# Four stages of a two-block network changed, and attention's outputs scaled in place of its probabilities

## The chip, the cores and the metric

One core of one Trainium2 chip. The time is the device time of one execution in microseconds.

## The reference

A sequence of 512 tokens of width 1024 goes through two blocks of two layers each. Both layers of the first block project the normed input, mix it in three ways side by side, and end with a feed-forward part:

```python
y_a, v_first = rwkv7_mixer(p_a, ...)      # state per head: S*w + sa (kk*a) + v k;  y = S r
# y is centred and scaled per head: (y - mean) * rsqrt(var + eps) * gn_w + gn_b
y_b = retention_mixer(p_b, positions)
y_c = mla_mixer(p_c, ...)                 # 8 heads: softmax(q k) @ v, causal
h = h + mix @ w_out[l]
h = h + (silu(gate) * up) @ w_down[l]
```

The second block has an even layer (rg_lru with gates sigmoid(u @ gate_w + b), 2 x 2 matrices of 128x128 for each of 8 heads, and a short convolution) and an odd layer (gated linear attention; its input gives q and k of 512 columns each). All is float32.

## The kernel before

Activations stand transposed: 128 features by 512 tokens in a tile of the arena, A(n); R(n) is the same memory as fp32r. A large product is made from two parts of each operand, high (ScalarE's rounded copy) and low (VectorE's difference): `product` issues three fp32r matmuls (L705 to L707). `gemm` (L731) is a plain fp32 product, which the trace shows as two records. Weights come in slabs of up to 128x2048 through two ring places; `prepare` splits a slab on ScalarE (L1555) and VectorE (L2142), and a slab may take a ring place of parts when the products of the slab two before it are done (slab_group). Each engine runs an order written out by hand; PSUM banks rotate, and `group` waits until the bank's last reader has released it.

What the change touches, in order of time:

- Start: TensorE's first product waits for the first half slab's parts (L2254).
- Attention, `mla(l)`: 32 units (8 heads, 4 blocks of queries). TensorE computes unit u's scores, VectorE their maximum in place (L2400, the custom operation), ScalarE the exponential with the row sums (L1699). VectorE then takes the sum's reciprocal (L2411) and scales the unit (L2413); three units later TensorE transposes it (L867), waiting for rows_scaled; ScalarE or VectorE (T_OWNER) copies it out, and `attended` (L845) multiplies with the values per pair of heads. VectorE's scans for rwkv stand after units 8 and 16, and a subtraction after unit 24. Behind the loop come kks (the sums behind L1683's squares), retention's scores with VectorE's masks (L2463), and `removal_key` between the two halves of these masks.
- rwkv: `token_tiles` turns the values (L1001); at the end ymean, a subtraction (L2588), squares (L1785), yvar. `beside(n)` places n products of the output projection.
- Even layer, `rg_gates(m)`, m = 0 to 7: four fp32 products.
- Between the layers: the last even_out tile and the odd layer's input are done in two token halves (`last_output`, `half_root`, `odd_input`). Products with odd_qk0's columns stand beside the parts of each k, those with odd_qk1's behind them; odd_qk1 is split in the ring amid odd_input.

## Time and profile before

| | us |
| --- | --- |
| median of 3 runs | 1994.52 (1991.6 to 1994.92) |
| the profiled execution | 1991.63, its span 1989.8 |
| TensorE busy (matmuls) | 1934.5, 97% of the span, 12070 instructions |
| VectorE busy | 1100.2, 55% |
| ScalarE busy | 832.7, 42% |
| HBM | 82 GB/s over the span |

Times in the rows are us from the span's start. PE is TensorE, DVE VectorE, ACT ScalarE, POOL GpSimd, SP the DMA queue's engine. Matmul records overlap: their ends are modelled, and the distance from start to start tells the rate.

### The profile page before, as it was taken

The page shows a single profiled execution, that of the slowest core. Times are in us where ns is not written, and L with a number is a line of the kernel's source. Part 1 is how long each engine was busy: PE and PEld are TensorE (multiplying, and loading weights), DVE is VectorE, ACT ScalarE, POOL GpSimd, SP SyncE. Part 2 cuts the span into 40 slices and gives each one's busy share as a digit, 9 for nine tenths or more (in the row PEclk, how much of TensorE's full clock was granted, in tenths as well). Part 3 has the DMA queues.
Part 4 walks back from the last instruction along what each step waited for, and adds up shares of the span by engine and source line. Part 5 has one row for each costly group of instructions (what it writes and reads, how often), then busy time and mean ns, then how long its engine had stood idle before and what let it go on. Part 6 is the DMA issues. An engine that isn't in the chain of part 4 may idle for free.

```text
span 1989.8 us, 28365 instructions
## 1 busy us (share of the span) xinstructions
PE 1934.5 (97%) x12070; PEld 1562.4 (79%) x12070; DVE 1100.2 (55%) x1585; ACT 832.7 (42%) x1206; POOL 41.7 (2%) x34
## 2 busy tenths in 40 slices
PE   7999899999999999998999999999999999999998
PEld 6875678888888888657788888887787777799887
DVE  6567846543444544876644334457676674443474
ACT  5257534322223313773432222245554653335273
POOL 0100000000000000000000000000000000020000
PEclk9999999999999999999999999999999999999999
DMA  6240003322322323201132233233212222212102
GB/s 236 94 125 1 24 24 106 106 80 101 106 99 73 114 88 111 63 1 46 64 106 93 84 109 106 73 108 127 101 69 106 85 74 96 100 63 95 64 16 81
DMA packets 28268, 170.01 MB, mean 85 GB/s; under 512 B 3632, under 2 KB 3888, under 8 KB 12912
## 3 DMA queue, kind: packets, MB, share of 16 engines
q1 hardware_dynamic: 28144, 168.21, 24.4%
q8 instruction: 96, 1.57, 0.3%
q14 instruction: 28, 0.23, 0.0%
HBM read 161.77 MB, written 2.10 MB: 82 GB/s over the span
## 4 chain that ended last, share of the span: by engine, by line
PE 88%; DVE 7%; ACT 3%; issue 1%; DMA 0%; SPq 0%; DVEq 0%; ACTq 0%
PE accumulators L705 26%; PE accumulators L707 25%; PE accumulators L706 25%; PE accumulators L731 4%; DVE ring_low L2142 1%; ACT arena L1652 1%; PE accumulators L845 1%; DVE accumulators L2400 1%; ACT ring_high L1555 1%; DVE arena L2413 1%; DVE arena L2463 1%; PE accumulators L1420 1%; PE accumulators L1439 1%; PE accumulators L953 1%; PE accumulators L987 1%
## 5 line engine op out<-in xcount | busy, mean ns | idle before, releaser
L705 PE MATMUL accumulators<-arena_split,ring_high 128*128 128x512 f32 (+1 forms) x2212 | 864.4, 391 | 18.2 <-DVE ring_low L2254 10.4
L706 PE MATMUL accumulators<-arena_split,ring_high 128*128 128x512 f32 (+1 forms) x2212 | 852.4, 385 | 0.0
L707 PE MATMUL accumulators<-arena_split,ring_low 128*128 128x512 f32 (+1 forms) x2212 | 852.4, 385 | 0.0
L705 PEld LDWEIGHTS accumulators<-arena_split,ring_high 128*128 128x128 f32 x2212 | 416.7, 188 | 110.6 <-DVE ring_low L2254 10.4
L706 PEld LDWEIGHTS accumulators<-arena_split,ring_high 128*128 128x128 f32 x2212 | 416.8, 188 | 86.0 <-issue 4.8
L707 PEld LDWEIGHTS accumulators<-arena_split,ring_low 128*128 128x128 f32 x2212 | 416.7, 188 | 83.5
L1555 ACT ACTIVATE ring_high<-ring 128x2048 fp32r<-128x2048 f32 (+3 forms) x161 | 281.5, 1749 | 405.5 <-PE accumulators L707 403.6
L2142 DVE TENSOR_TENSOR ring_low<-ring,ring_high 128x2048 fp32r<-128x2048 f32 (+3 forms) x161 | 336.9, 2093 | 185.5 <-ACT ring_high L1555 184.8
L1573 ACT ACTIVATE arena<-accumulators 128x512 f32<-128x512 f32 x72 | 43.1, 598 | 277.2 <-DVE accumulators L2123 277.1
L2123 DVE TENSOR_TENSOR accumulators<-accumulators,rstd 128x512 f32<-128x512 f32 x72 | 50.3, 699 | 118.8 <-PE accumulators L707 118.8
L2622 DVE TENSOR_TENSOR arena<-arena,accumulators 128x512 f32<-128x512 f32 x44 | 30.3, 688 | 119.6 <-PE accumulators L707 118.1
L2149 DVE TENSOR_TENSOR arena_split<-arena,arena_split 128x512 fp32r<-128x512 f32 x94 | 62.1, 690 | 53.8 <-ACT arena_split L1561 53.6
L731 PE MATMUL accumulators<-arena 128*128 128x512 f32 (+8 forms) x256 | 85.3, 482 | 2.5 <-DVE arena L2463 2.5
L1523 ACT ACTIVATE arena<-accumulators 128x512 f32<-128x512 f32 (+1 forms) x76 | 43.3, 596 | 93.5 <-PE accumulators L707 50.3
L705 PE MATMUL accumulators<-ring_high,arena_split 128*128 128x352 f32 (+2 forms) x240 | 82.1, 342 | 0.0
L707 PE MATMUL accumulators<-ring_high,arena_split 128*128 128x352 f32 (+2 forms) x240 | 80.9, 337 | 0.0
L706 PE MATMUL accumulators<-ring_low,arena_split 128*128 128x352 f32 (+2 forms) x240 | 80.8, 337 | 0.0
L731 PEld LDWEIGHTS accumulators<-arena 96*128 96x128 f32 (+2 forms) x256 | 38.3, 189 | 30.9 <-issue 16.5
L1561 ACT ACTIVATE arena_split<-arena 128x512 fp32r<-128x512 f32 x94 | 55.4, 622 | 17.0 <-DVE arena L2596 6.5
L2117 DVE TENSOR_TENSOR arena<-accumulators,rstd 128x512 f32<-128x512 f32 x40 | 27.6, 689 | 46.6 <-PE accumulators L707 46.5
L1567 ACT ACTIVATE arena<-h 128x512 f32<-128x512 f32 x32 | 20.1, 629 | 66.5 <-DVE h L2193 66.5
L705 PEld LDWEIGHTS accumulators<-ring_high,arena_split 128*128 128x128 f32 x240 | 45.0, 188 | 3.6 <-issue 0.2
(362 smaller groups left out, 1722.0 us busy)
## 6 DMA issues: line engine op xcount, KB each, us to landing
ring<-slabs_in SPq DMA_DIRECT2D x115, 1024.0 KB, 4.8
ring<-slabs_in SPq DMA_DIRECT2D x38, 704.0 KB, 4.0
ring<-slabs_in SPq DMA_DIRECT2D x4, 576.0 KB, 3.5
h<-x_in SPq DMA_DIRECT2D x4, 512.0 KB, 7.6
con<-con_in SPq DMA_DIRECT2D x1, 2048.0 KB, 9.3
arena<-arena SPq DMA_DIRECT2D x8, 256.0 KB, 4.1
arena<-arena SPq DMA_DIRECT2D x32, 64.0 KB, 2.5
out<-arena SPq DMA_DIRECT2D x8, 256.0 KB, 2.0
```

Of the source, the lines that this page charges most:

```text
L705: pe.matmul(out, weight[0], right[0], start=start, stop=False)
L706: pe.matmul(out, weight[0], right[1], start=False, stop=False)
L707: return pe.matmul(out, weight[1], right[0], start=False, stop=stop)
L731: mm = pe.matmul(b[out_rows, 0:N], w, r, start=(k == 0), stop=(k == len(weights) - 1))
L1523: f(dst, b[rows, 0:n], func, scale=scale).then_inc(cnt.up(act_released), 1)
L1555: f(ring_high[:, n % SLOTS, 0:cols], ring[:, at % SLOTS, 0:cols], ACT.Copy).then_inc(cnt.up(slab_high_ready), 1)
L1561: f(R(dst), src, ACT.Copy).then_inc(cnt.up(high_ready), 1)
L1573: f(dst, bank(key)[:, :], ACT.Silu).then_inc(cnt.up(act_released), 1)
L2123: tt(b[:, :], b[:, :], rstd[:, :], MUL).then_inc(cnt.up(scaled_ready), 1)
L2142: tt(ring_low[:, n % SLOTS, 0:cols], ring[:, at, 0:cols], ring_high[:, n % SLOTS, 0:cols].bitcast(F32), SUB).then_inc(cnt.up(slab_split), 1)
L2149: tt(R(dst), src, R(high).bitcast(F32), SUB).then_inc(cnt.up(parts_ready), 1)
L2622: tt(a, A(j % 2)[:, 0, :], b[:, :], MUL).then_inc(cnt.up(dve_released), 1)
```

## The change

Five edits. (1) VectorE writes a tile of zeros first, and TensorE multiplies it with itself seven times (ZERO_PRODUCTS = 7) into the last bank, before its first product. (2) The gates' weights and inputs are split into high and low parts, held in three tiles over the decay constants, and `rg_gates` uses `split_gemm`. (3) rwkv's values are turned by a product with a centring matrix (identity minus the mean over 64) in place of a transpose; the mean's sums and subtraction go, and squares are taken from PSUM. (4) odd_qk1 is split early, into half tiles of the arena in place of the ring (`early_high`, `early_low`), and all four banks are filled k by k. (5) The probabilities aren't scaled. For each pair of heads VectorE writes 512 reciprocals of the sums (4 blocks x 2 heads x 64 equal columns), TensorE transposes them (`spread_factors`), ScalarE copies them out, and VectorE multiplies the pair's output with them as it leaves PSUM (`scaled_values`). VectorE now also copies the transposed third block.

The diff, cut to its core (plain lines of context and new semaphores are left out):

```diff
@@ -128,6 +128,7 @@
     put("ones64", same)
+    put("centre64", np.eye(P) - same / RW_HD)
...
@@ -366,7 +367,9 @@
         arena_split = nc.alloc_sbuf_tensor_at("arena_split", [P, 53, T], F32R, offset=arena_at)
+        con_at = nc.sbuf_base
         con = sb("con", [P, NCON])
+        gate_parts = nc.alloc_sbuf_tensor_at("gate_parts", [P, 3, T], F32R, offset=-(-(con_at + 4 * CON["decay"][0]) // 32) * 32)
...
@@ -612,7 +628,12 @@
         TOKENS = (slice(0, T // 2), slice(T // 2, T))
-        T_OWNER = ("dve", "act", "act", "act")
+        def half_weights(places, k):
+            tile, at = places[k // 2]
+            return R(tile)[:, at + k % 2 * P:at + k % 2 * P + P]
+        T_OWNER = ("dve", "act", "dve", "act")
...
@@ -845,8 +866,17 @@
                     if blocks[-1] == NT - 1:
-                        enter(key, "act")
+                        enter(key, "dve")
                         mm.then_inc(psum_ready, 1)
+                def spread_factors(pair_of):
+                    pe.wait_ge(sums_inverted, cnt.next(sums_inverted))
+                    b = group(("factor", l, pair_of), "act")
+                    for j in range(NT):
+                        js = slice(j * P, (j + 1) * P)
+                        mm = pe.transpose(b[:, js], A(4 + pair_of)[:, 0, js], cst("ident"))
+                    mm.then_inc(psum_ready, 1)
...
@@ -860,7 +890,7 @@
                         w = u - 3
-                        pe.wait_ge(rows_scaled, cnt.next(rows_scaled))
+                        pe.wait_ge(*taken(("s", l, w)))
...
@@ -868,6 +898,9 @@
                         attended((u - 13) // 8, VALUE_UNITS[(u - 13) % 8])
+                    if u >= 12 and u % 8 == 4 and u < len(units):
+                        spread_factors((u - 12) // 8)
+                spread_factors(MLA_H // 2 - 1)
...
@@ -1003,7 +1036,12 @@
                 pe.wait_ge(values_ready, cnt.next(values_ready))
-                token_tiles(0, 14)
+                for hp in range(2):
+                    b = group(("tok", l, 0, hp), "act")
+                    for j in range(NT):
+                        js = slice(j * P, (j + 1) * P)
+                        mm = pe.matmul(b[:, js], A(14 + hp)[:, 0, js], cst("centre64"), start=(j == 0), stop=(j == NT - 1))
+                    mm.then_inc(psum_ready, 1)
...
@@ -1124,16 +1162,16 @@
                 mm.then_inc(outputs_ready, 2)
-                beside(2)
+                beside(3)
+                pe.wait_ge(y_squares_ready, cnt.next(y_squares_ready, 2))
                 for hp in range(2):
-                    for s in range(2):
-                        pe.wait_ge(*taken(("y", l, s)))
-                    gemm(("ymean", l, hp), "dve", rows, [cst("ones64")], [A(49 + hp)[:, 0, :]])
-                beside(1)
-                for hp in range(2):
-                    pe.wait_ge(y_squares_ready, cnt.next(y_squares_ready))
+            pe.wait_ge(zeros_ready, 1)
+            zeros = A(50)[:, 0, :]
+            for n in range(ZERO_PRODUCTS):
+                pe.matmul(banks[BANKS - 1][:, :], zeros[:, 0:P], zeros, start=True, stop=True)
...
@@ -1232,14 +1270,10 @@
             def rg_gates(m):
-                if m < 2:
-                    pe.wait_ge(first_gates_loaded, 16)
-                else:
-                    pe.wait_ge(gates_loaded, 16)
-                pe.wait_ge(conv_ready, cnt.next(conv_ready))
+                pe.wait_ge(gate_parts_ready, cnt.next(gate_parts_ready, 2))
                 for n in range(4):
-                    w = A(m)[:, 0, n * P:(n + 1) * P]
-                    gemm(("gate_ri", m, n // 2, n % 2), "act", rows, [w], [A(19 + m % 2)[:, 0, :]])
+                    w = gate_part(GATE_HIGH)[:, n * P:(n + 1) * P], R(m)[:, n * P:(n + 1) * P]
+                    split_gemm(("gate_ri", m, n // 2, n % 2), "act", [w], [(gate_part(INPUT_HIGH), gate_part(INPUT_LOW))])
...
@@ -1280,15 +1314,16 @@
             for n in range(4):
-                w = split_tiles(split_slab("odd_qk0"), n % 2 * DT * P, DT) if n < 2 else None
+                if n < 2:
+                    w = split_tiles(split_slab("odd_qk0"), n % 2 * DT * P, DT)
+                else:
+                    pe.wait_ge(slab_split, split_index["odd_qk1"] + 1)
+                    w = [(half_weights(QK1_HIGH, n % 2 * DT + k), half_weights(QK1_LOW, n % 2 * DT + k)) for k in range(DT)]
                 bk, w = held[n]
-                if w is None:
-                    w = split_tiles(split_slab("odd_qk1"), n % 2 * DT * P, DT)
-                    held[n] = bk, w
...
@@ -1296,24 +1331,13 @@
-            for k in range(DT):
-                parts_step(k)
-                for n in range(2):
-                    odd_product(n, 0, k)
-                if k == 2:
-                    half_norm_sum(1)
-            later = [(n, half, k) for half in range(2) for k in range(DT) for n in (2, 3)]
-            for n, half, k in later[:2 * DT]:
-                odd_product(n, half, k)
-            del later[:2 * DT]
-            for k in range(DT):
-                parts_step(k)
-                for n in range(2):
-                    odd_product(n, 1, k)
-                if k < 4:
-                    odd_product(*later.pop(0))
-            for n, half, k in later:
-                odd_product(n, half, k)
+            for half in range(2):
+                for k in range(DT):
+                    parts_step(k)
+                    for n in range(4):
+                        odd_product(n, half, k)
+                    if half == 0 and k == 2:
+                        half_norm_sum(1)
...
@@ -1688,9 +1712,8 @@
                           ACT.Copy).then_inc(cnt.up(act_released), 1)
-                    last = 14 + max(VALUE_UNITS)
-                    if u >= last and (u - last) % 8 == 0 and (u - last) // 8 < MLA_H // 2 - 1:
-                        copy_out(("pv", l, (u - last) // 8), A(4 + (u - last) // 8)[:, 0, :])
+                    if u >= 13 and u % 8 == 5 and u < MLA_H * NT:
+                        copy_out(("factor", l, (u - 13) // 8), A(4 + (u - 13) // 8)[:, 0, :])
...
@@ -1699,6 +1722,7 @@
+                copy_out(("factor", l, MLA_H // 2 - 1), A(3 + MLA_H // 2)[:, 0, :])
...
@@ -1716,8 +1740,6 @@
                     act.preload_act_table_set(ROOTS)
-                copy_out(("pv", l, MLA_H // 2 - 1), A(3 + MLA_H // 2)[:, 0, :])
...
@@ -1754,6 +1776,7 @@
                     if n == 3:
+                        act.wait_ge(*taken(("pv", l, MLA_H // 2 - 1)))
...
@@ -1778,11 +1801,13 @@
                     b = bank(("y", l, s))
+                    squares = A(51, 2).rearrange("p h (j s t) -> p (h j) s t", s=2, t=RW_CHUNK)
+                    f(squares[:, :, s, :], b[:, :].rearrange("p (j t) -> p j t", t=RW_CHUNK), ACT.Square).then_inc(
+                        cnt.up(y_squares_ready), 1)
+                for s in range(2):
+                    b = bank(("y", l, s))
                     f(dst[:, :, s, :], b[:, :].rearrange("p (j t) -> p j t", t=RW_CHUNK), ACT.Copy).then_inc(cnt.up(act_released), 1)
-                for hp in range(2):
-                    act.wait_ge(*taken(("ymean", l, hp)))
-                    f(A(51 + hp)[:, 0, :], A(49 + hp)[:, 0, :], ACT.Square).then_inc(cnt.up(y_squares_ready), 1)
...
@@ -1873,14 +1898,27 @@
+            def gate_highs(m):
+                if m < 2:
+                    act.wait_ge(first_gates_loaded, 16)
+                else:
+                    act.wait_ge(gates_loaded, 16)
+                f(gate_part(GATE_HIGH), A(m)[:, 0, :], ACT.Copy).then_inc(cnt.up(gate_high_ready), 1)
+                act.wait_ge(conv_ready, cnt.next(conv_ready))
+                f(gate_part(INPUT_HIGH), A(19 + m % 2)[:, 0, :], ACT.Copy).then_inc(cnt.up(gate_high_ready), 1)
                 prepare(f"even_xb_gc{m}")
+                if m == 0:
+                    gate_highs(0)
                     gate_silu(m + 1)
+                    gate_highs(m + 1)
...
@@ -1911,6 +1949,16 @@
+            def early_high(first, last):
+                at = slab_index["odd_qk1"]
+                act.wait_ge(slab_loaded[at % SLOTS], 16 * (at // SLOTS + 1))
+                src = ring[:, at % SLOTS, :].rearrange("p (a t) -> p a t", t=T // 2)[:, first:last]
+                (tile, start), count = QK1_HIGH[first], last - first
+                f(arena_split[:, tile:tile + count, start:start + T // 2] if tile > 25 else
+                  R(tile)[:, start:start + count * T // 2].rearrange("p (a t) -> p a t", t=T // 2), src, ACT.Copy).then_inc(
+                    cnt.up(early_high_ready), 1)
...
@@ -1936,14 +1984,16 @@
+            early_high(5, 7)
+            early_high(7, 8)
             last_output(0)
+            early_high(0, 5)
+            splits.append("odd_qk1")
                     last_output(1)
-                if m == 2:
-                    prepare("odd_qk0")
...
@@ -2154,6 +2204,7 @@
+            dve.memset(A(50)[:, 0, :], 0.0).then_inc(zeros_ready, 1)
...
@@ -2391,6 +2442,13 @@
+                def scaled_values(pair_of):
+                    dve.wait_ge(psum_ready, finished(("pv", l, pair_of)))
+                    dve.wait_ge(*taken(("factor", l, pair_of)))
+                    y = A(4 + pair_of)[:, 0, :]
+                    tt(y, bank(("pv", l, pair_of))[:, :], y, MUL).then_inc(cnt.up(dve_released), 1)
...
@@ -2405,12 +2463,13 @@
                            bank(("t", l, w))[:, 0:(i + 1) * P].rearrange("p (j t) -> p j t", t=P)).then_inc(cnt.up(dve_released), 1)
-                    w = u - 1
-                    if 0 <= w < MLA_H * NT:
-                        dve.wait_ge(*taken(("s", l, w)))
-                        dve.reciprocal(stat[:, 3, w:w + 1], stat[:, 2, w:w + 1]).then_inc(cnt.up(dve_done), 1)
-                        dve.wait_ge(cnt.sem, cnt.value)
-                        ts(probabilities(w), probabilities(w), stat[:, 3, w:w + 1], None, MUL).then_inc(cnt.up(rows_scaled), 1)
+                    if u >= 18 and u % 8 == 2 and (u - 18) // 8 < MLA_H // 2 - 1:
+                        scaled_values((u - 18) // 8)
+                    if u >= 9 and u % 8 == 1:
+                        dve.wait_ge(*taken(("s", l, u - 2)))
+                        factors = A(4 + (u - 9) // 8)[:, 0, :].rearrange("p (j e c) -> p e j c", j=NT, e=2)
+                        sums = stat[:, 2, u - 9:u - 1].rearrange("p (e j) -> p e j", j=NT)[:, :, :, None]
+                        dve.reciprocal(factors, sums.broadcast_to((P, 2, NT, 64))).then_inc(cnt.up(sums_inverted), 1)
...
@@ -2463,6 +2522,7 @@
                     if hp == 0:
+                        scaled_values(MLA_H // 2 - 1)
...
@@ -2582,11 +2642,6 @@
                 for hp in range(2):
-                    dve.wait_ge(psum_ready, finished(("ymean", l, hp)))
-                    b = bank(("ymean", l, hp))
-                    y = A(49 + hp)[:, 0, :]
-                    stt(y, b[:, :], -1.0 / RW_HD, y, MUL, ADD).then_inc(cnt.up(dve_released), 1)
-                for hp in range(2):
...
@@ -2717,10 +2772,20 @@
+            def gate_lows(m):
+                dve.wait_ge(gate_high_ready, cnt.next(gate_high_ready))
+                tt(R(m), A(m)[:, 0, :], gate_part(GATE_HIGH).bitcast(F32), SUB).then_inc(cnt.up(gate_parts_ready), 1)
+                dve.wait_ge(gate_high_ready, cnt.next(gate_high_ready))
+                tt(gate_part(INPUT_LOW), A(19 + m % 2)[:, 0, :], gate_part(INPUT_HIGH).bitcast(F32), SUB).then_inc(
+                    cnt.up(gate_parts_ready), 1)
                 prepare(f"even_xb_gc{m}")
+                if m == 0:
+                    gate_lows(0)
...
@@ -2737,6 +2802,8 @@
                 tt(yb, b[:, :], c, MUL).then_inc(cnt.up(dve_released), 1)
+                if m < DT - 1:
+                    gate_lows(m + 1)
...
@@ -2798,8 +2865,20 @@
+            def early_low(dst, first, last, high):
+                src = ring[:, slab_index["odd_qk1"] % SLOTS, :].rearrange("p (a t) -> p a t", t=T // 2)[:, first:last]
+                dve.wait_ge(early_high_ready, cnt.next(early_high_ready))
+                return tt(dst, src, high.bitcast(F32), SUB)
             last_square(0)
-            odd_input(0, {3: lambda: last_square(1), 4: lambda: prepare("odd_qk0")})
+            as_halves = lambda view: view.rearrange("p (a t) -> p a t", t=T // 2)
+            dve.wait_ge(psum_ready, finished(("eo", DT - 1, 0)))
+            early_low(arena_split[:, 14:16, TOKENS[0]], 5, 7, as_halves(R(24))).then_inc(cnt.up(dve_done), 1)
+            early_low(as_halves(R(25)[:, TOKENS[0]]), 7, 8, as_halves(R(25)[:, TOKENS[1]])).then_inc(cnt.up(dve_done), 1)
+            early_low(arena_split[:, 9:14, TOKENS[0]], 0, 5, arena_split[:, 26:31, TOKENS[0]]).then_inc(cnt.up(slab_split), 1)
+            splits.append("odd_qk1")
+            odd_input(0, {3: lambda: last_square(1)})
```

## Rows read from the trace of the kernel before

**Rows 1.** The page, part 4: shares of the chain that ended last, by engine.

```profile
PE 88%; DVE 7%; ACT 3%; issue 1%; DMA 0%; SPq 0%; DVEq 0%; ACTq 0%
```

**Rows 2.** Waits of TensorE: waiter, awaited: us in all, times, longest.

```profile
PE accumulators L867 <- DVE arena L2413: 6.3, 16, 0.6
```

**Rows 3.** First 17 us, timeline: start, us, engine line operation [idle before, awaited].

```profile
0.81 0.17 DVE L2158 MEMSET epsilon<- 128x1 f32 x5 [0.81 <-PEq L3097]
...
10.39 0.79 PE L705 MATMUL accumulators<-arena_split,ring_high 128*128 128x512 f32 x1 [10.39 <-DVE ring_low L2254]
...
15.64 0.39 PE L705 MATMUL accumulators<-arena_split,ring_high 128*128 128x512 f32 x1
```

**Rows 4.** Chain in time (start, us, what), and VectorE's timeline: one gate stage.

```profile
1469.70 3.43 PE accumulators L731 x8
...
1505.79 3.43 PE accumulators L731 x8
...
1500.57 0.69 DVE L2739 TENSOR_TENSOR arena<-accumulators,arena 128x512 f32<-128x512 f32 x1
```

**Rows 5.** Timeline of TensorE where the odd layer's q and k are projected.

```profile
1732.02 0.35 PE L705 MATMUL accumulators<-arena_split,ring_high 128*128 128x256 f32 x1 [0.63 <-DVE arena_split L2796]
...
1738.88 0.39 PE L705 MATMUL accumulators<-arena_split,ring_high 128*128 128x256 f32 x1 [2.94 <-DVE arena_split L2796]
...
1757.01 0.29 PE L707 MATMUL accumulators<-arena_split,ring_low 128*128 128x256 f32 x1
1757.13 0.28 PE L705 MATMUL accumulators<-arena_split,ring_high 128*128 128x256 f32 x1
...
1761.81 0.50 PE L705 MATMUL accumulators<-arena_split,ring_high 128*128 128x512 f32 x1 [0.20 <-DVE ring_low L2142]
```

**Rows 6.** There: busy times, granted clock (0.50), DMA share, GB/s; then ScalarE, VectorE.

```profile
1740.00:1742.00 2.00, 2.00 (x10) 1.99 (x10) 1.82 (x6) 2.00 (x7) 0.00 (x0) 0.50 0.92 389
...
1757.39 1.92 ACT L1555 ACTIVATE ring_high<-ring 128x2048 fp32r<-128x2048 f32 x1 [5.82 <-PE accumulators L707]
...
1759.35 2.41 DVE L2142 TENSOR_TENSOR ring_low<-ring,ring_high 128x2048 fp32r<-128x2048 f32 x1 [7.57 <-ACT ring_high L1555]
...
1729.53 0.88 DVE L2788 SCALAR_TENSOR_TENSOR arena<-arena,par 128x256 f32<-128x256 f32 x2 [3.38 <-ACT arena L1930]
```

**Rows 7.** Timeline of TensorE in layer 0's rwkv: the means, and the token tiles.

```profile
279.01 1.88 PE L731 MATMUL accumulators<-arena,con 128*128 128x512 f32 x4
...
218.28 1.97 PE L1001 MATMUL accumulators<-con,arena 128*128 128x128 f32 x16
```

**Rows 8.** Two lines' instructions, the reciprocals: count: ns min/median/max, first and last start.

```profile
L2411 DVE RECIPROCAL stat<-stat x64: 152/159/165, 153.4 to 859.4; 128x1 f32<-128x1 f32 x64
...
L2225 DVE RECIPROCAL splus<-splus x1: 253/253/253, 348.1 to 348.1; 128x16 f32<-128x16 f32 x1
```

**Rows 9.** Timelines inside layer 0's attention loop: VectorE, TensorE, VectorE, ScalarE.

```profile
171.89 1.22 DVE L2387 TENSOR_TENSOR_SCAN arena<-con,arena 128x512 f32<-128x512 f32 x1
...
176.28 0.55 PE L867 MATMUL accumulators<-con,arena 128*128 128x128 f32 x3 [0.52 <-DVE arena L2413]
...
178.71 0.57 DVE L2400 CUSTOM_DVE_ANT_0 accumulators<-accumulators,con 128x384 f32<-128x384 f32 x1 [0.52 <-PE accumulators L731]
...
179.90 0.19 ACT L1699 ACTIVATION_READ_ACCUMULATOR arena<-accumulators,stat 128x1 f32 x1
```

**Rows 10.** Timelines behind the attention loops of layers 0 and 1 (from 859).

```profile
192.05 0.19 ACT L1699 ACTIVATION_READ_ACCUMULATOR arena<-accumulators,stat 128x1 f32 x1
...
195.18 1.12 PE L731 MATMUL accumulators<-arena,con 128*128 128x512 f32 x2 [1.33 <-ACT arena L1683]
...
204.38 1.29 DVE L2463 TENSOR_TENSOR arena<-accumulators,con 128x512 f32<-128x512 f32 x2 [1.53 <-PE accumulators L731]
...
859.16 0.19 ACT L1699 ACTIVATION_READ_ACCUMULATOR arena<-accumulators,stat 128x1 f32 x1
...
862.72 0.70 PE L731 MATMUL accumulators<-arena,con 128*128 128x512 f32 x1
```

14 lines of the change are left out of this document (12 added, 2 removed).

## The prediction

> **What bounds the kernel now.** I read four views in this order. The chain of work that ended last says who holds the end: TensorE does, for 88% of the span [rows 1]. So an edit that takes TensorE work away shortens the run by that work, unless a wait takes its place, and the waits of TensorE come next. They are short and few; the group that this change is after is the transposes of attention (L867), which wait 16 times for VectorE's scaling of the probabilities, 6.3 us in all [rows 2]. A record is longer than the slot its matmul takes: 256 columns show 0.28 us at 0.12 us apart [rows 5]. A wait is therefore some 0.16 us longer than its record says, and those 16 waits are worth 6.3 + 16 x 0.16 = 8.9 us. Third, the timeline at the places that the diff touches. Last, the granted clock of the one stretch in which the spacing of equal matmuls doubles.
>
> **Zero products at the start.** TensorE first works at 10.39, when the first half slab is split; twelve matmuls of 512 columns pass before 15.64, from where they stand closer [rows 3]. In the stage of the gates 144 such matmuls take 36.09 - 3.43 = 32.66 us, 0.227 each [rows 4]. The twelve took 5.25 us and would take 2.72 at that rate: **-2.5 us** if the array is awake by then. VectorE writes the zeros ahead of its memset at 0.81 [rows 3], so TensorE starts about 1.2. A plain fp32 product of 512 columns costs 2 x 0.429 = 0.86 us at the full rate (eight records in 3.43 [rows 4]) and twice that at half. Three at 1.71 and four at 0.86 end near 9.8, ahead of 10.39. If the clock never rose they would end at 13.2, and this would be +2.8 instead. What is late next is the next slab, whose transfer and parts have a few us of room; I take the full 2.5. The Trainium skill ("TensorE: Matmul & The Clock Gate", The HAM clock gate) states that the throttled state is the default and activity releases it, which would give the same sum.
>
> **Gates in parts.** For each of eight m, four fp32 products (eight records, 3.43 us) become twelve fp32r ones, 12 x 0.227 = 2.72: -0.71 each, **-5.7 us** in all. It costs two copies on ScalarE and two subtractions on VectorE for each m (0.5 to 0.7 us each). They are in time: VectorE ends its product with gb at 1501.2, the two subtractions would end at 1502.5, and TensorE wants them at 1505.79 [rows 4]. TensorE sets the pace of this stage with no wait at all, so nothing is behind them; without this cover it would be 1.3 us for each m.
>
> **Centred values.** The two sums for the mean of y go, with the VectorE and ScalarE steps that hung on them: 4 records of 0.43, 1.71 us, and some 0.14 of switching [rows 7]. The squares are ready before the three products that now stand beside them are done. In turn, eight of the sixteen transposes at 218.28 become fp32 products of two records each, 8 x 0.11 = 0.87 us, and TensorE goes on to the next step without a wait, so this is on the path. Net -1.0 for each layer, **-2.0 us**. The bounds are -1.85 x 2 (the 0.87 hidden) and 0.
>
> **The qk slab in half tiles.** Before, 64 half products were cut by the split of odd_qk1, which stands in the middle of the parts. TensorE stood 2.94 us before 1738.88 [rows 5], and then ran at a clock of 0.50 of full, the 1.2 GHz level, for some 3.4 us [rows 6]. After, all 192 matmuls run from 1732.02 in one stream: 192 x 0.12 = 23.0, and 0.4 for the norm sum. VectorE's part of a k comes every 1.13 us (0.44 + 0.34 + 0.35), TensorE's takes 1.44, so no wait is left inside. The early split costs VectorE 2.35 us (2.41 us for 2048 columns), which fit into its 3.38 us of idle before 1729.53 [rows 6]. But the new order ends all four banks together. The split of odd_qk2 needs the ring place of odd_qk0, free only when bank qk1 is done, now the last k. From the last matmul of qk1 at 1757.01 it takes 4.80 us until the next pair starts at 1761.81: ScalarE's copy from 1757.39, VectorE's subtraction from 1759.35 [rows 5, 6]. Before, qk2 and qk3 covered that for all but 0.36; now seven matmuls do, 0.84 us. The next pair starts at 1732.02 + 23.4 + 4.80 - 0.84 = 1759.4, so -2.4. An idle time of 3.9 us is longer than the one that ended at 1738.88, and I expect the clock to fall again, half of 3.4 us: +1.7. **-0.7 us**; bounds -2.4 and 0.
>
> **Attention: outputs scaled in place of probabilities.** Per layer, 32 small reciprocals and 32 scalings leave VectorE, and TensorE's transposes wait for the exponential alone: the waits go, -8.9 / 2 = -4.5. Four groups of four transposes come (spread_factors), 0.11 each and 0.1 of switching: three in the loop, +1.5. VectorE gets one reciprocal of 512 elements for each pair of heads. Its price is not in the trace, its slope is: 128x1 takes 159 ns, 128x16 takes 253 [rows 8], (253 - 159) / 15 = 6.3 ns an element, so 159 + 511 x 6.3 = **3.35 us**. The bounds are 0.69 (a product of 512 elements [rows 4]) and 253 / 16 x 512 = 8.1; I take the slope, since both rows are of this operation and share a fixed cost. This is what the change turns on. The scores' maximum of the next unit is queued behind this reciprocal, and TensorE waits for it twice: at the factors' transposes and at the next unit's.
> Unit 17 [rows 9]: VectorE's scan would start 0.6 earlier than 171.89, since the scaling ahead of it is gone. The scan holds the engine 1.1 us, the maximum of unit 17 some 0.35 (256 columns, against 0.57 for the 384 of 178.71), so the reciprocal runs from 172.75 to 176.1. TensorE reaches the factors at 176.28 - 0.68 - 0.43 = 175.2 and stands 1.0. Factors and score end at 177.05. Unit 18's maximum starts at 176.1; from its start to its exponential's end is 1.4 (178.71 to 180.09), so the transposes start near 177.6 and not 176.28: 0.5 more. Pair 2 is like it. For unit 9 fewer products lie between and it stands 2.1 + 0.45. Together 5.5 a layer. The loop: -4.5 + 1.5 + 5.5 = +2.5, +5.0 for two layers.
> Behind the loop: the last reciprocal starts when unit 31's exponential ends (192.24) and ends at 195.6; the factors take until 196.15, and the sums that started at 195.18 come after them, +1.0 [rows 10]. In layer 1 nothing was waited for here, so there is no room to hide in: the exponential ends at 859.35, the reciprocal would end at 862.7, the factors at 863.2, vlow takes 1.83, and the sums that started at 862.72 start at 865.0, +2.3. Then scaled_values of the last pair stands ahead of removal_key on VectorE and waits for pv; VectorE was idle 1.53 us before 204.38, where the next masks start [rows 10]. TensorE ends pv right before the products of those masks, about 1.1 us ahead of 204.38; 203.3 + 0.6 (scaled_values) + 1.35 (removal_key) = 205.25, +0.9 in each layer, and from there VectorE holds the path. Behind the loop +5.1. Attention: **+10.1 us**.
>
> **Sum.** -2.5 - 5.7 - 2.0 - 0.7 + 10.1 = -0.8 us. The profiled execution took 1991.63 us, its span 1989.8, with 1.8 around it; the median of the three shown is 1994.52, and the changes of a span carry over. Profiled 1990.8; against the median **1993.7 us**.
>
> **Rivals.** *The reciprocal is cheap* (a 512-element pass like any other, 0.69): no stall is left in the loop, -6.0 for two layers; behind it -1.0 (the squares come earlier), +0.5 and 2 x 0.9, +1.3. Attention -4.7, the sum -15.6, 1978.9 us. Against it stands the slope of 6.3 ns, where a product of 512 elements takes 1.3 an element. *The stalls cost the clock, slower*: TensorE stands 2.1 us at unit 9 and 2 us before the last factors, in each layer, where now it stands 0.5 at most and 1.5. If half the rate follows each of the four, as after 1738.88, that is 4 x 1.7 = +6.8: 2000.5 us. It decides from the point at which 2 us of standing is enough; 2.94 is shown to be. For it: the matmuls around are short. Against it: the 1.33 us before 195.18 left the clock up. The longer reciprocal ends at the same place: each us on it costs 8 us over both layers, and from 4 us on the kernel is slower by over 0.2%. *The stalls are half*: VectorE runs ahead of TensorE by a unit, since 0.6 us a unit is gone from it, and no clock falls at odd_qk2: -2.7 - 1.7, 1989.3 us. *The zero products don't wake the array* or end late: +2.5 to +5.3, 1996 to 1999 us.
>
> **How the numbers follow.** Forecast 0.58; cheap reciprocal 0.13; half stalls 0.12; clock or a longer reciprocal 0.14; zeros useless 0.03. About 0.2%, 4 us, is what a measurement of this kernel can tell from no change. Around the forecast the bounds of centred values and qk make some 4 us each way: 0.12 of its 0.58 lies under 1990.5, 0.03 over 1998.5. Faster 0.12 + 0.13 + 0.11 = 0.36, slower 0.03 + 0.13 + 0.01 = 0.17, same 0.47. The range runs from 1984 to 2001, which leaves out the cheap reciprocal and the ends, 2 in 10; the forecast's own is 1989 to 1998.
>
> **What the profile after would show.** First real matmuls 0.227 apart at 10.4; gate stages 35.4 long; one RECIPROCAL line of 128x512 x8 with a mean near 3350 ns, and L867's successor waiting for the maximum (the custom operation) and for it; a gap of 3.9 us ahead of odd_qk2; masks of the second retention half waiting for removal_key. The forecast is wrong first of all if that mean is not 3.3, then if the gap or the clock after it is not there.

## The result

The changed kernel takes 2006.3 us (median of four runs, 2004.8 to 2010.0), the kernel before 1994.7 us (1991.6 to 1996.5): ratio 1.0065, 95% interval 1.0048 to 1.0081. It is slower by about 12 us. The forecast was 1993.7 with a range from 1984 to 2001, so the range did not hold it. The profiled run took 2004.8 us, its span is 2003.0 and that of before 1989.8: 13.2 us to explain, where the sum said -0.8.

To place them I took equal TensorE instructions of the two traces and subtracted their starts. This is how far the changed kernel is behind (+) or ahead (-) at each point, by the time of the kernel before:

```
place (time of before)               lag us   stage adds   the prediction's sum
first slab done (20 to 140)           -2.4      -2.4         -2.5
layer 0 done (280)                    -0.3      +2.1  \
layer 1 done (960)                   +15.2     +15.5  /      +8.1 for both
gates and recurrence done (1620)     +12.5      -2.7         -5.7
qk and the wait behind it (1780)     +11.8      -0.7         -0.7
rest of the odd layer (1850)         +13.2      +1.4          0
```

Two stages came as forecast, one gave half, one cost 1.4 where nothing was changed, and the two layers took 17.6 in place of 8.1. This is one execution of each kernel; a second profile of the changed kernel (changed_again, below) has +6.4 in layer 0 and +15.2 in layer 1, so the 2.1 of layer 0 is at the low end. The waits of TensorE in the changed kernel (engine line, the one waited for, us in total, times, longest) answer to [rows 2]:

```profile
PE accumulators L878 <- DVE arena L2472: 8.5, 4, 2.1
PE accumulators L878 <- DVE ring_low_plain L2464: 7.7, 4, 2.0
PE accumulators L986 <- DVE arena L2601: 5.8, 6, 1.7
PE accumulators L726 <- DVE ring_low L2192: 3.9, 1, 3.9
PE accumulators L938 <- DVE arena L2522: 2.8, 2, 2.4
...
PE accumulators L1091 <- issue: 2.4, 2, 1.6
...
PE accumulators L726 <- DVE gate_parts L2780: 2.1, 1, 2.1
PE accumulators L986 <- issue: 2.0, 1, 2.0
...
PE accumulators L1148 <- issue: 1.5, 1, 1.5
```

L878 is the factors' transposes: eight waits, 16.2 us, in place of the sixteen of 6.3 us at L867. Only four of them end with the reciprocal (L2472). The other four end with L2464, VectorE's copy of turned probabilities. The group of the reciprocal, which answers to [rows 8], from the groups by line (count | busy us, mean ns | idle before):

```profile
L2472 DVE RECIPROCAL arena<-stat 128x512 f32<-128x512 f32 x8 | 26.8, 3349 | 1.5 <-ACT arena L1722 1.5
```

3349 ns where 3350 was forecast: the price was right, what it holds up was not. VectorE at unit 17, then TensorE beside it (start, length, and in brackets the idle time before and what ended it), answer to [rows 9]:

```profile
168.76 1.21 DVE L2438 TENSOR_TENSOR_SCAN arena<-con,arena 128x512 f32<-128x512 f32 x1
169.90 0.41 DVE L2458 CUSTOM_DVE_ANT_0 accumulators<-accumulators,con 128x256 f32<-128x256 f32 x1
170.22 0.14 DVE L2458 DVE_READ_ACCUMULATOR2_ANT stat<- 128x1 f32 x1
170.22 3.35 DVE L2472 RECIPROCAL arena<-stat 128x512 f32<-128x512 f32 x1
173.48 0.54 DVE L2458 CUSTOM_DVE_ANT_0 accumulators<-accumulators,con 128x384 f32<-128x384 f32 x1
173.94 0.14 DVE L2458 DVE_READ_ACCUMULATOR2_ANT stat<- 128x1 f32 x1
173.94 0.55 DVE L2464 COPY ring_low_plain<-accumulators 128x384 f32<-128x384 f32 x1
```

```profile
1.45 9.19 PE L1174 MATMUL accumulators<-arena 128*128 128x512 f32 x14 [1.45 <-DVE arena L2207]
10.07 0.80 PE L726 MATMUL accumulators<-arena_split,ring_high 128*128 128x512 f32 x1
10.71 0.40 PE L727 MATMUL accumulators<-arena_split,ring_high 128*128 128x512 f32 x1
...
172.41 0.38 PE L897 MATMUL accumulators<-con,arena 128*128 128x128 f32 x2
174.64 1.09 PE L878 MATMUL accumulators<-con,arena 128*128 128x128 f32 x4 [1.85 <-DVE ring_low_plain L2464]
```

The reciprocal ends at 173.57, but TensorE goes on at 174.64: behind the reciprocal stand a maximum and the copy that empties the bank which the factors' transposes are to get. From there the matmuls are long (four transposes 1.09 where 0.63 to 0.66 is usual), because the clock fell at that moment. The upper rows of the fence are the start, [rows 3] of before: the first real product starts at 10.07, the second 0.64 behind it, and from 10.71 on they stand 0.23 apart.

The granted clock in two stretches of the changed kernel (length, busy us and count of each engine, then the clock):

```profile
849.00:853.40 4.40, 4.40 (x29) 2.83 (x26) 3.80 (x9) 2.23 (x8) 0.00 (x0) 1.00 0.00 0
857.30:860.70 3.40, 3.40 (x10) 1.27 (x9) 0.97 (x7) 2.34 (x8) 0.00 (x0) 0.50 0.00 0
```

The second follows the wait of 2.00 that ends at 856.4. Besides one at the very end of either, the trace of before has two stretches at half the clock (1.2 GHz) and this one has eight, of 3.4 us each: four at waits for VectorE in attention (174.6, 198.5, 857.3, 867.5), two in the short products of layer 1 (932.4, 959.7; 1 to 2 us behind waits marked "issue" of 2.02 and 1.50), one ahead of odd_qk2 (1772.0), and one at 1840.3. Before the last one stand these rows:

```profile
1836.98 2.00 PE L1383 MATMUL accumulators<-con,arena 64*128 64x64 f32 x32
1838.91 1.16 PE L1370 MATMUL accumulators<-small,arena 17*128 17x128 f32 x16
1840.00 0.43 PE L726 MATMUL accumulators<-ring_high,arena_split 128*128 128x352 f32 x1
1840.27 0.46 PE L727 MATMUL accumulators<-ring_low,arena_split 128*128 128x352 f32 x1
```

TensorE did not stand at all, it ran 3 us of small products (64 and 17 rows high). The same products in the kernel before left the clock up. That is the 1.4 us of the last stage. It is no single event: small_reciprocal, a kernel of the next section, lost the clock at the same products, again with no wait ahead of them, and the other eleven profiles did not.

```profile
1815.24 1.16 PE L1370 MATMUL accumulators<-small,arena 17*128 17x128 f32 x16
1816.33 0.48 PE L726 MATMUL accumulators<-ring_high,arena_split 128*128 128x352 f32 x1
```

### The profile page after: what moved, and what is told of

It is laid out like the page before. It is cut to its first block, busy times and chain, and to the rows that moved or that the text cites. A ratio compares the mean times of both kernels' runs of the same rounds, so it can differ in the third digit from the quotient of the medians.

```text
span 2003.0 us, 28469 instructions
## 1 busy us (share of the span) xinstructions
PE 1943.0 (97%) x12156; PEld 1579.5 (79%) x12156; DVE 1117.4 (56%) x1504; ACT 833.3 (42%) x1208; POOL 42.1 (2%) x34
## 3 DMA queue, kind: packets, MB, share of 16 engines
q8 instruction: 97, 1.59, 0.3%
## 4 chain that ended last, share of the span: by engine, by line
PE 90%; DVE 7%; ACT 2%; issue 2%; DVEq 0%; ACTq 0%
PE accumulators L726 26%; PE accumulators L728 26%; PE accumulators L727 26%; PE accumulators L752 3%; DVE ring_low L2192 1%; DVE arena L2472 1%; PE accumulators L866 1%; PE accumulators L969 1%; PE accumulators L986 1%; PE accumulators L1444 1%; PE accumulators L1463 1%; DVE arena_split L2199 1%; DVE arena L2522 1%; PE accumulators L1020 1%; ACT ring_high L1579 0%
## 5 line engine op out<-in xcount | busy, mean ns | idle before, releaser
L726 PE MATMUL accumulators<-arena_split,ring_high 128*128 128x512 f32 (+1 forms) x2180 | 851.4, 391 | 7.9 <-DVE ring_low L2192 3.9
L728 PE MATMUL accumulators<-arena_split,ring_low 128*128 128x512 f32 (+1 forms) x2180 | 842.8, 387 | 0.0
L727 PE MATMUL accumulators<-arena_split,ring_high 128*128 128x512 f32 (+1 forms) x2180 | 842.7, 387 | 0.0
L726 PEld LDWEIGHTS accumulators<-arena_split,ring_high 128*128 128x128 f32 x2180 | 410.2, 188 | 97.8 <-DVE ring_low L2192 5.9
L727 PEld LDWEIGHTS accumulators<-arena_split,ring_high 128*128 128x128 f32 x2180 | 410.4, 188 | 84.6 <-issue 2.6
L728 PEld LDWEIGHTS accumulators<-arena_split,ring_low 128*128 128x128 f32 x2180 | 410.2, 188 | 83.4
L1547 ACT ACTIVATE arena<-accumulators 128x512 f32<-128x512 f32 (+2 forms) x76 | 43.3, 596 | 99.1 <-PE accumulators L728 50.3
L752 PE MATMUL accumulators<-arena 96*128 96x128 f32 (+5 forms) x192 | 57.4, 452 | 2.0 <-DVE arena L2522 1.5
L1722 ACT ACTIVATE arena<-accumulators,stat 128x128 f32<-128x128 f32 (+1 forms) x64 | 33.6, 531 | 36.4 <-issue 20.6
L727 PEld LDWEIGHTS accumulators<-ring_low,arena_split 128*128 128x128 f32 x240 | 45.7, 190 | 3.3 <-issue 0.2
```

Of the source, the lines that this page charges most:

```text
L726: pe.matmul(out, weight[0], right[0], start=start, stop=False)
L727: pe.matmul(out, weight[0], right[1], start=False, stop=False)
L728: return pe.matmul(out, weight[1], right[0], start=False, stop=stop)
L752: mm = pe.matmul(b[out_rows, 0:N], w, r, start=(k == 0), stop=(k == len(weights) - 1))
L1547: f(dst, b[rows, 0:n], func, scale=scale).then_inc(cnt.up(act_released), 1)
L1722: f(probabilities(u), bank(("s", l, u))[:, 0:(u % NT + 1) * P], ACT.Exp, bias=stat[:, 1, u:u + 1], scale=-1.0, accum_out=stat[:, 2, u:u + ...
```

## Experiments

All kernels were run in three groups, each on another chip; each group ran the kernel before beside them (median 1993.2, 1994.7 and 1992.9 us: the first four rows, the next four, the last three). The ratios stand against the kernel before of the same group. "The lag" below is always what the first table of the result shows: the start of equal TensorE instructions in two traces, subtracted.

```
kernel                          us       ratio to before, 95%
attention_alone                 2014.5   1.0102 [1.0085, 1.0118]
without_attention_edit          1981.5   0.9943 [0.9928, 0.9958]
small_reciprocal                1981.4   0.9939 [0.9924, 0.9954]
filled_waits                    2006.9   1.0066 [1.0049, 1.0083]
removal_key_first               1979.3   0.9919 [0.9903, 0.9936]
all_mended                      1972.4   0.9889 [0.9875, 0.9904]
mended_without_attention_edit   1977.1   0.9908 [0.9893, 0.9923]
code_shifted                    1982.2   0.9929 [0.9911, 0.9947]
half_reciprocal                 1991.2   0.9993 [0.9984, 1.0003]
changed_again                   2007.2   1.0069 [1.0052, 1.0086]
cheap_attention_alone           1983.4   0.9954 [0.9939, 0.9969]
```

### The attention edit alone, and everything but it

attention_alone is the kernel before with the hunks of the diff that touch attention.

> The kernel before with the attention edit alone: factors by one reciprocal of 512 elements, spread by transposes, outputs scaled in place of probabilities. Theory: the attention edit carries all of the loss. In the two profiles the two layers grew by 2.1 and 15.5 us, and the centred values take some 2 us off, so this kernel is +18 to +20 us, near 2013 us, with eight waits of about 2 us for the reciprocal and at least four stretches at half the clock. Rival: the growth of the second layer (four stretches at half rate and 4 us in which TensorE waits for nothing the profile shows) comes from the other edits, above all the centred values, which moved the instructions behind attention. Then this kernel is +6 to +12 us, 2001 to 2007 us.

without_attention_edit is the changed kernel with those hunks taken back.

> The changed kernel with attention as it was: zero products, gates in parts, half tiles of the qk slab, centred values. Theory: -2.4 (start) - 2.9 (gates with one wait of 2.1) - 2 (centred values) - 0.7 (qk) = -8, near 1987 us. Rival, that the second layer's growth lies in the centred values and in where the instructions come to stand: 1992 us or more, with waits of TensorE of 1 to 2 us behind attention that no engine ends.

Measured: 2014.5 (+21.3) and 1981.5 (-11.7). The attention edit carries the whole loss and more, the theory holds. On top of the other four edits it costs about what it costs alone: 23.3 (from -11.7 to +11.6, each against its own kernel before) and 21.3. Its waits are the changed kernel's to the tenth:

```profile
PE accumulators L857 <- DVE arena L2432: 8.5, 4, 2.1
PE accumulators L857 <- DVE ring_low_plain L2424: 7.7, 4, 2.0
PE accumulators L917 <- DVE arena L2482: 2.8, 2, 2.4
```

The clock fell at seven of the eight waits at L857. The other four edits gave more than the 8 us expected: against before they stand at -2.7 behind the start, -7.3 behind layer 0, -8.6 behind layer 1, -11.4 behind the gates, -10.8 behind qk. Layer 0 gave 4.6 and not 1.0, because before has there a stretch at half clock (247.7) and 5.0 us of waits marked "issue", and this kernel none and 3.4. Layer 1 gave 1.3, with a clock fall of its own in it (863.4).

### A small reciprocal

```
-dve.reciprocal(factors, sums.broadcast_to((P, 2, NT, 64)))            # 128x512
+dve.reciprocal(stat[:, 3, u-9:u-1], stat[:, 2, u-9:u-1])              # 128x8
+dve.wait_ge(cnt.sem, cnt.value)
+cp(factors, sums.broadcast_to((P, 2, NT, 64)))     # sums now views row 3
```

> The changed kernel with the reciprocal taken of the 8 sums (128x8) and then copied out to the 512 elements, in place of one reciprocal of 512. Theory: the reciprocal's 3.35 us are what TensorE waits for (eight waits of 1.85 to 2.12 us) and these waits are what takes the clock down (four of the eight falls of the profile). With 0.2 + 0.7 us in its place the waits shrink to 0.3 or less: -14, and the four falls go: -6.8, near 1985.5 us. Rival: the clock falls come from the products being short, not from the waits; then -14 alone, 1992 us. Second rival: what is behind the reciprocal on VectorE is late anyway; then not under 2000 us.

Measured 1981.4, 25 us under the changed kernel. The copy takes 0.43 us. No wait at L878 is left and no stretch at half clock lies in the loops; the same holds for the four other kernels with the small reciprocal, which run the same short products there. So the short products alone don't take the clock at these places. Between the two traces the lag steps at each of the eight places, in layer 0 by 2.7, 3.6, 2.3 and 3.5 us: the 3.6 and the 3.5 are the two behind which the clock fell. In layer 1 the steps are 2.7, 2.1, 4.0 and 3.8, the last two with the clock. So one such wait of 1.85 to 2.12 costs 2.1 to 2.7 us, and 1 us or more on top where the clock falls; together 12.1 and 12.6 us. The longest waits that this kernel has left:

```profile
PE accumulators L986 <- DVE arena L2603: 5.8, 6, 1.7
PE accumulators L726 <- DVE ring_low L2192: 3.9, 1, 3.9
PE accumulators L1091 <- issue: 2.8, 2, 2.0
PE accumulators L938 <- DVE arena L2524: 2.8, 2, 2.5
```

### Half the reciprocal

The reciprocal goes over 32 of each 64 columns, a copy makes the others.

> The changed kernel with the reciprocal of 256 elements and a copy for the other 256: 159 + 255 x 6.3 = 1.77 us and 0.35, about 2.15 with the wait between them, where the changed kernel has 3.35 and small_reciprocal 0.63. Theory (a threshold: TensorE has 1.2 us of slack at these places, since it waits 2.12 for 3.35): eight waits of some 0.9 us and no clock fall at them, 8 us over small_reciprocal, near 1989.5 us. Rival (each us of the reciprocal costs alike from the first): 24.6 x (2.15 - 0.63) / (3.35 - 0.63) = +13.7, near 1995 us.

Measured 1991.2, between the two but nearer the threshold's 1989.5 than the rival's 1995. The reciprocal and the waits for it:

```profile
L2472 DVE RECIPROCAL arena<-stat 128x256 f32<-128x256 f32 x8 | 14.0, 1748 | 1.5 <-ACT arena L1722 1.5
```

```profile
PE accumulators L878 <- DVE arena L2474: 3.4, 4, 0.9
PE accumulators L878 <- DVE ring_low_plain L2464: 2.7, 4, 0.7
```

1748 ns for 256 and 3349 for 512: 6.25 ns an element, the slope of [rows 8]. The eight waits are 0.59 to 0.85 us, so TensorE has 1.2 to 1.5 us of room there, and the clock fell behind none of them. In layer 0 they cost 1.4, 0.9, 1.1 and 1.0 against small_reciprocal, in layer 1 4.1 together: 8.5 of the 9.8 us between the two medians, where the theory said 8 and the rival 13.7. One of its stretches, 6.8 us long (864.2), stands 1.6 us behind another wait, of 0.98.

### Filling the waits

```
 def spread_factors(pair_of):
-    pe.wait_ge(sums_inverted, ...)
     b = group(("factor", l, pair_of), "act")
+    for n in range(2):
+        pe.matmul(b[:, :], cst("ident"), cst("carry"), start=True, stop=True)
+    pe.wait_ge(sums_inverted, ...)
```

> The changed kernel with two plain fp32 products of 512 columns (0.86 us each at the full clock) ahead of each wait for the reciprocal; they go into the bank that the factors' transposes overwrite. The waits of 2 us are as long as before, but TensorE works in them. Theory (the waits cost the clock): the stretches at half rate at these waits go, four in the profile, up to -6.8 us, near 1999.5 us. Rival (the clock falls there whatever TensorE does): no change, 2006 us, or +1 to +3 where the products outlast a wait.

Measured 2006.9, no change, and my expectation was built on a wrong picture: in the middle two pairs of each layer TensorE waits inside group(), for the bank, before it reaches the fillers.

```profile
174.66 3.63 PE L876 MATMUL accumulators<-con 128*128 128x512 f32 x4 [1.76 <-DVE ring_low_plain L2466]
178.08 0.69 PE L880 MATMUL accumulators<-con,arena 128*128 128x128 f32 x4
```

There the fillers (L876) come after a wait of 1.76 and add their own 1.7 to 3.6 us. At the other four places they filled it (four waits of 0.4 are left of 8.5 us), and the clock did not fall directly behind them, where it fell at 8 of the 12 unfilled waits of this kind in the three profiles with the long reciprocal (attention_alone, the changed kernel and changed_again). Four places are few, and the middle waits could not be filled: the products need a bank, and TensorE waits for just that. So that work in a wait keeps the clock is made likely and not shown. What is shown is the count of the waits themselves: in those three profiles the clock fell at 4, 7 and 5 of eight waits of 1.85 us or more, 16 of 24; where the same places have waits of 0.59 to 0.85 (half_reciprocal) or none, at none of them.

### The changed kernel again

> The changed kernel once more, with nothing altered, for what of its profile stays and what moves. Theory: the waits stand at the same instructions with the same lengths within 0.1 us (eight of 1.85 to 2.12 for the reciprocal, 2.45 in retention of layer 1, 2.07 at gates(1), 3.86 ahead of odd_qk2), the stretches at half rate are between 8 and 13 and lie at other ones of these waits; each is worth 1 to 1.7 us between runs. Rival: the clock falls at the same places each time, and the runs differ by something else.

Measured 2007.2. The waits repeat:

```profile
PE accumulators L878 <- DVE arena L2472: 8.5, 4, 2.1
PE accumulators L878 <- DVE ring_low_plain L2464: 7.7, 4, 2.0
```

and so do those of 2.45, 2.07 and 3.86. The half-clock stretches do so in part: 162.6, 176.3, 189.9, 835.0 (6.8 us long), 872.6, 937.4, 1418.7, 1777.1, 1913.6, where the first profile had the eight named above. Four of the nine (176.3, 872.6, 937.4, 1777.1) stand at the same waits as in the first profile (174.6, 867.5, 932.4, 1772.0), the other five at new places. So neither the theory (at other waits) nor the rival (at the same ones) holds as it was put: some of the places change from run to run, and the share of the eight waits too. The waits marked "issue" are not quite fixed either: 8.4 us in the first profile, 9.7 in this one, which has one of 1.67 in layer 0 (279.1) that the first has not. Over the runs of this kernel the mean granted clock goes from 0.993 to 0.989 as the span goes from 2003.0 to 2008.2 us.

### VectorE and GpSimd meet

In layer 1 the mask wait (L938) is 2.45 us, in layer 0 it is 0.35, by the same code. VectorE and then GpSimd of small_reciprocal:

```profile
858.82 0.69 DVE L2450 TENSOR_TENSOR arena<-accumulators,arena 128x512 f32<-128x512 f32 x1 [3.71 <-PE accumulators L866]
859.43 3.50 DVE L2485 SCALAR_TENSOR_TENSOR arena<-arena,par 128x512 f32<-128x512 f32 x2
862.85 3.26 DVE L2524 TENSOR_TENSOR arena<-accumulators,con 128x512 f32<-128x512 f32 x8
```

```profile
859.78 2.59 POOL L3061 TENSOR_TENSOR arena<-arena 128x1024 f32<-128x1024 f32 x1 [117.73 <-ACT arena L1741]
862.45 2.69 POOL L3063 TENSOR_TENSOR arena<-arena 128x1024 f32<-128x1024 f32 x1
```

removal_key (L2485, two products) now stands behind scaled_values (L2450), and so meets the mixing of values, which GpSimd does in layer 1 alone. The second product took 2836 ns, its sisters 744 to 747. removal_key_first exchanges two lines:

```
 if hp == 0:
-    scaled_values(MLA_H // 2 - 1)
     removal_key()
+    scaled_values(MLA_H // 2 - 1)
```

> small_reciprocal with removal_key ahead of the last scaled_values on VectorE, two lines exchanged. In layer 1 of small_reciprocal the second product of removal_key (860.09) took 2836 ns and not 747; it lies inside the first product of GpSimd (859.78, 2594 ns), and TensorE then stands 2.45 us for the masks of retention. Theory: the new place behind scaled_values let the two meet. Exchanged, both products take 0.75, the wait of 2.45 shrinks to 0.5 or less, in layer 1 alone: -2 us, and up to 1.7 more where the clock no longer falls there; 1978 to 1979.5 us. Rival: the masks wait for scaled_values itself, which still stands ahead of them: 0 to -0.5.

Measured 1979.3, -2.1; the two medians come from different groups (-15.4 and -11.8 against their own kernel before), and their intervals overlap, so the time alone tells nothing and the traces carry the verdict. L2485 there (min, median, max of ns):

```profile
L2485 DVE SCALAR_TENSOR_TENSOR arena<-arena,par x4: 739/743/747, 193.6 to 852.6; 128x512 f32<-128x512 f32 x4
```

The wait at L938 is gone, and against small_reciprocal the lag falls by 4.2 us around it: the wait of 2.45 and a stretch at half clock that small_reciprocal had right behind it (864.2). But 3.3 had been lost just before, in a stretch of 6.8 us at half clock of its own (852.8). So the cause of the long product and of the wait is shown; that the exchange shortens the run is not. The Trainium skill ("SBUF — State Buffer", SBUF: two separate sides) says that VectorE with two SBUF inputs and GpSimd take one pair of ports in turn, each for a whole instruction. The rows agree: the product of 747 lasts until the GpSimd instruction that began during the one before it is over, 859.78 + 2.59 = 862.37, and 0.55 more. GpSimd's two are longer too, 2.59 and 2.69, where removal_key_first has 2.35 for both.

### Instruction loading

TensorE's waits marked "issue" are 7.2 us in before, 8.4 in the changed kernel, all among the short 64x64 products of the two layers. The page of the profile shows a queue that loads instructions (q8, 97 loads, 1.59 MB), and in such stretches one comes every 4 to 5 us, among the long products one every 28. In the thirteen profiles there are 58 such waits of over 0.7 us, and every one of them ends 1.2 to 1.6 us after the transfer of a load is over. So these waits end with loads; that is more than nearness, since the loads are 4 to 5 us apart.

> small_reciprocal with one zero product less at the start and 96 waits more in TensorE's program there, on a semaphore that is already up: the same work, other places of the instructions in the blocks of 16384 bytes that the instruction queue loads. TensorE of small_reciprocal stood 1.98 us in layer 0 and 1.03, 1.74, 0.84, 0.36 and 1.50 in layer 1 with no engine ending it, each beside such a load. Theory: these waits belong to the places of the block borders; they move to other instructions and their sum changes, by 1 us or more in either layer. Rival: they belong to the instructions at which they stand (a long queue, a switch); then they stay at the same lines with the same lengths. The time moves by at most 3 us either way.

Measured 1982.2, equal to small_reciprocal. Rows of TensorE between 900 and 925 that begin behind such a wait, first of small_reciprocal, then of code_shifted:

```profile
908.14 0.45 PE L986 MATMUL accumulators<-arena 64*64 64x64 f32 x13 [1.74 <-issue]
921.15 0.33 PE L1091 MATMUL accumulators<-arena 64*64 64x64 f32 x3 [0.84 <-issue]
924.76 0.45 PE L969 MATMUL accumulators<-arena 64*64 64x64 f32 x14 [0.36 <-issue]
```

```profile
900.94 0.56 PE L986 MATMUL accumulators<-arena 64*64 64x64 f32 x20 [0.27 <-issue]
909.16 0.53 PE L995 MATMUL accumulators<-con,arena 128*128 128x128 f32 x2 [2.66 <-issue]
923.29 0.81 PE L1091 MATMUL accumulators<-arena 64*64 64x64 f32 x25 [1.77 <-issue]
```

They moved to other instructions and lengths (1.03 at L969 and 1.50 at L1148 went too), with the same work behind the start. Without the shift they mostly stay: of the six that the changed kernel has in layer 1, five stand at the same lines in changed_again, with lengths within 0.4 us. So the places belong to where the instructions lie in the program. Their sum changed less than I expected: 7.6 us and 8.1, of which layer 0 has 2.2 in both. One thing came beside it: with six zero products in place of seven TensorE stood 1.97 us ahead of the first real product, the clock fell at 11.7, and the start was 1.6 us later.

### The mended kernels

```
+if m == 0: gate_lows(1)      # ahead of prepare(even_gb_zb0), not behind
 ...
-for n in range(4):                          # qk, second half
-    odd_product(n, half, k)
+for n in range(2):
+    odd_product(n, half, k)
+if k >= 4:
+    for n in (2, 3): odd_product(n, half, k - 4)
 ...                                         # the last four k of qk2, qk3 behind the loop
```

> removal_key_first with two more edits: the two subtractions for gates(1) ahead of the next slab's split on VectorE (TensorE stood 2.07 us for them), and in the second half of qk the products of qk2 and qk3 four k behind those of qk0 and qk1, so that the bank that frees the ring's place for odd_qk2 is done 24 products earlier (TensorE stood 3.9 us). Theory: -2.1 and -2.9 with a fall of the clock less, -1.7: some -5 to -6.5 against removal_key_first, 1973 us. Rival: the subtractions delay the split by 1.3 us and the wait only moves; the products of qk0 and qk1 wait for their parts when they stand alone: then -1 to -2.

> without_attention_edit with the same two edits at gates(1) and at qk. Theory: as above, -5 to -6.5 against 1981.5, 1975.5 us; the attention edit with the cheap reciprocal is then worth the difference to all_mended, -2.5 (loop -6, back behind the loops). Rival: the attention edit is worth nothing even so, and the two kernels are equal within 1 us.

Measured 1972.4 and 1977.1. all_mended is the fastest kernel here, 22 us under the one before. The wait at gates(1) is gone, and that ahead of odd_qk2 fell from 3.9 to 1.3 with no clock fall:

```profile
PE accumulators L726 <- DVE ring_low L2198: 2.0, 2, 1.3
```

(Its two are 1.28 at qk and 0.73 in the gates.) Between removal_key_first and all_mended the lag falls by 2.3 at gates(1), 1.0 of it comes back at once as the wait of 0.73 for the split that now comes later, and by 3.6 at qk. So of my rival "the wait only moves" some four tenths came true at gates(1). The two kernels lie 4.7 us apart, what the attention edit is worth beside the others once its reciprocal is cheap; 2.5 was expected. In the two profiles 1.3 of it stands there before attention begins, so that part is none of the edit's. Against mended_without_attention_edit the lag of all_mended falls by 5.0 and 3.3 us in the two loops and 2.2 more behind the first; 6.9 come back behind the second, where all_mended has three stretches at half clock (851.9 for 6.8 us, 906.6, 933.9) and the other kernel one.

### The attention edit, cheap and alone

> The kernel before with the attention edit alone, the reciprocal of 8 sums copied out, and removal_key ahead of the last scaled_values. Theory: the loops give back what the change was after (32 waits for the scaling gone, factors' transposes added: -3 a layer in the prediction's terms), and nothing is lost behind them: -4 to -7, near 1988 us. Rival: what comes behind the loops is held by the masks and by the loading of instructions, and takes the gain back: 1993 us, no change.

Measured 1983.4, -9.5 against its own kernel before, more than expected. The profiled execution is its slowest, 6.0 under the profiled one of before. By its trace layer 0 gives 4.8 us and layer 1 3.3; two stretches at half clock in the odd layer take 2.4 back. The edit is worth twice as much alone as beside the others (4.7); no run tells why. attention_alone and this kernel differ in the reciprocal and in two exchanged lines, and lie 31 us apart.

## Why the prediction was wrong, step by step

The prediction's signs of being wrong did not warn: the mean of the reciprocal, the gap ahead of odd_qk2 and the clock after it all came as said. What it had wrong it had not put among the signs.

**Zero products**: right, -2.4 for -2.5; the other profiles with seven of them have -2.0 to -3.3, and the two kernels without any -0.8 and -0.2, so a single profile tells this to about half a us. **The qk slab**: right, -0.7, with a gap of 3.86 for 3.9 and a fall of the clock at it. Where that stretch was 6.8 us long (without_attention_edit, half_reciprocal) the stage cost 0.6 and 0.3 instead. Both had every term in a row.

**Gates in parts**: each is 0.62 us shorter (36.09 to 35.47 for a stage), 0.71 was said. The other 2.1 us is one wait, at gates(1). The step that failed is "They are in time: ... [rows 4]". Those rows are of a later m. For m = 0 the gates stand behind the xb/gc pair, so gates(1) comes only 27 us after gates(0) and not 35.5, and the two subtractions stand behind a split of 2.2 us. I read a steady stage and did not look at its first turn.

**Centred values**: no run has them alone. Layer 1 of without_attention_edit shows -1.3 with other effects in it, which agrees with the -1.0 said and does not measure it.

**Attention**: that TensorE would stand for the reciprocal was right, and so was its length, 3.35 us (the sum as written, 159 + 511 x 6.3, gives 3.38; the measured mean is 3.349). The stalls were still too small, since for half of them the wait was another than the one priced. Three terms failed.

First, the waits. For units 17 and 25 the text has TensorE stand 1.0 for the factors and 0.5 at the next unit. It stood 1.85 and 2.00, since it waited for the bank that VectorE's copy empties, behind reciprocal and maximum. T_OWNER gives every fourth unit to VectorE in place of ScalarE; the diff says so, and I gave this line no price. No run puts that line back, so how much hangs on it alone is open. My charge for the four places of a layer was 2.55, 1.5, 1.5 and 2.0 (from -1.0 with no wait to +1.0); the lag against small_reciprocal, less an estimated 1 us where the clock fell, gives 2.7, 2.6, 2.3 and 2.5 in layer 0. This is 2.5 us a layer, and the unit that I worked out with all its rows at hand, unit 9, is the one that came out right.

Second, the clock. It was a rival: "*The stalls cost the clock, slower*", four falls, 2000.5 us. I gave it 0.14 (together with a longer reciprocal), against it "the 1.33 us before 195.18 left the clock up". 1.33 is not 2, and there were eight waits of 2 us and not four; in three profiles 16 of 24 lost it. One row that left the clock up was no evidence either: over the thirteen profiles the clock fell within 3.2 us behind a wait of 0.98 among short products (layer 1's L752) in seven, and behind one of 1.26 in the odd layer in six. Two falls lay in each layer's loop, some 2 us. Loops and last pair came to +7.7 and +9.2 where 3.5 and 4.8 were said, 4.2 and 4.4 too little: 2.5 from the waits and 2 from the clock.

Third, what stands behind. scaled_values ahead of removal_key was +0.9 a layer. In layer 0 the lag goes from 5.3 over 4.8 to 5.7 there, +0.4 (0.9 from its lowest). In layer 1 it goes from 8.9 over 7.9 to 10.6, +1.7 (2.7 from its lowest): the new place put removal_key beside GpSimd. "VectorE holds the path" was right, but the duration of an instruction in its old place was taken for its duration in a new one.

**Luck of the places**: behind these, layer 0 gave 6.0 us back (a clock fall of before gone, 2.85 less of issue waits, 1.0 of centred values, the rest small) and layer 1 lost 4.6 (4.1 more of issue waits and the two clock falls at 932.4 and 959.7, less 1.0). Apart from the forecast 1.0 a layer this is -5.0 and +5.6, which nearly cancel. No reading of the trace of before could have told them, but it shows that they exist (5.0 us of issue waits in layer 0 and 2.2 in layer 1 by the same code), and the range had nothing for them, nor for the 1.4 us of the last stage.

The other rivals: *the reciprocal is cheap*, 1978.9 us, is what small_reciprocal does; it took 1981.4, with the L938 wait on top. *The stalls are half* did not come: they were 1.85 to 2.12 us at all eight places. half_reciprocal halves them by other means and gives 1991.2.
## What to carry to other kernels

A long instruction on a shared engine costs not its length but what stands in its queue behind it: list each instruction behind it and each bank, not only the result it makes. Take such an operation over the few distinct values and copy them out. When an instruction moves, look what the other engines do at its new time, and look at the first turn of a loop by itself. A wait of 2 us among short products should be priced with the clock, here about 1 us more in two cases of three, and shorter waits are not safe: 0.98 us lost it in seven profiles of thirteen.
